# Router tiles transposed two chunks behind each product, their evacuation on ScalarE alone from tile 1 on, and SyncE's third weight load held until the first gather has landed

## What is computed

```python
def reference(x, mem, ...):
    mem_k, mem_v = project(_rms_norm(mem, norm_mem), xa_wkv)
    h = x
    for i in range(DEPTH):                                   # DEPTH = 2
        h = h + token_mixer(_rms_norm(h, norm_mix[i]))
        h = h + _memory_cross_attention(_rms_norm(h, norm_cross[i]), mem_k, mem_v, xa_wq[i], xa_wo[i])
        h = h + _hierarchical_moe(_rms_norm(h, norm_ffn[i]), moe_wg[i], moe_bg[i], moe_we[i], moe_be[i],
                                  moe_w1[i], moe_w3[i], moe_w2[i])
    return _rms_norm(h, norm_final)

def _hierarchical_moe(h, wg, bg, we, be, w1, w3, w2):        # 4 groups of 8 experts, D_EXPERT = 256
    g_logits = t @ wg + bg;  e_logits = t @ we + be
    # top-1 group, top-2 experts inside it, gate = softmax of the two times the group's probability
    for gi in range(G):
        hid = silu(t @ w1[gi]) * (t @ w3[gi]) * gate[gi]
        y = y + hid @ w2[gi]
```

## Time and profile before

| | us |
|---|---|
| median of 3 runs | 1807.48 (1802.3 to 1815.66) |
| the profiled execution | 1805.5 |
| its span, first to last instruction | 1803.6 |
| TensorE busy in the span | 1614.6 (90%) |
| VectorE, ScalarE, GpSimd busy | 708.1 (39%), 416.9 (23%), 164.5 (9%) |
| mean granted TensorE clock | 0.954 |

### The profile page before, as it was taken

The page is one execution under the profiler, slowest core; times in us unless marked ns, Lnnn a source line. Parts: engine busy times, 40 slices in busy tenths (PEclk is TensorE's granted clock), DMA queues, the critical chain, the costliest instruction groups (busy, mean ns, idle before and its releaser), DMA issues.

```text
span 1803.6 us, 26870 instructions
## 1 busy us (share of the span) xinstructions
PE 1614.6 (90%) x11581; PEld 845.2 (47%) x11581; DVE 708.1 (39%) x1308; ACT 416.9 (23%) x825; POOL 164.5 (9%) x185
## 2 busy tenths in 40 slices
PE   4999989998799999869887899999999996997876
PEld 2444458887464445434333344445544544333332
DVE  5310676664375215444221331205640454441215
ACT  2102335554300212211000120006511313010002
POOL 2000213330000000011111200000000000110101
PEclk8999999999799999879998999999999997998998
DMA  7119000000541611259999932211015025799994
GB/s 234 37 57 318 3 2 4 4 5 4 210 138 48 233 47 51 90 226 417 424 425 424 364 135 93 73 67 48 1 59 221 0 71 224 302 423 424 425 422 183
DMA packets 81496, 312.80 MB, mean 173 GB/s; under 512 B 17776, under 2 KB 18856, under 8 KB 56608
## 3 DMA queue, kind: packets, MB, share of 16 engines
q1 hardware_dynamic: 69280, 282.76, 40.0%
q0 software_dynamic: 10944, 24.10, 3.6%
q10 hardware_dynamic: 1152, 4.19, 0.6%
HBM read 305.81 MB, written 33.29 MB: 188 GB/s over the span
## 4 chain that ended last, share of the span: by engine, by line
PE 72%; issue 7%; DVE 4%; ACT 4%; DMA 1%; POOL 0%; another core or an unknown queue 0%; PEld 0%; DVEq 0%; ACTq 0%; POOLq 0%
PE PS L565 14%; PE PS L2269 14%; PE PS L605 10%; PE PS L1113 7%; PE PS L2294 6%; PE PS L579 5%; PE PS L1447 2%; PE PS L2254 2%; PE PS L2218 2%; PE PS L1423 1%; PE PS L1647 1%; PE PS L1668 1%; PE PS L504 1%; PE PS L1658 1%; PE PS L1814 1%
## 5 line engine op out<-in xcount | busy, mean ns | idle before, releaser
L565 PE MATMUL PS<-arena,ring 128*128 128x512 f32 (+1 forms) x1024 | 415.2, 567 | 0.0
L565 PEld LDWEIGHTS PS<-arena,ring 128*128 128x128 f32 x1024 | 195.4, 191 | 216.3 <-issue 210.7
L2269 PE MATMUL PS<-ring,arena 128*64 128x512 f32 x512 | 131.7, 673 | 50.8 <-issue 47.8
L605 PE MATMUL PS<-ring,arena 128*128 128x512 f32 x320 | 144.5, 602 | 0.7 <-ACT arena L1613 0.7
L2269 PE MATMUL PS<-arena 128*64 128x512 f32 x512 | 118.0, 614 | 15.0 <-issue 12.3
L2277 DVE TENSOR_TENSOR arena<-PS,arena 128x256 f32<-128x256 f32 x32 | 13.6, 424 | 249.6 <-PE PS L2284 231.0
L2269 PEld LDWEIGHTS PS<-ring,arena 128*64 128x64 f32 x512 | 43.6, 155 | 136.9 <-issue 133.2
L687 ACT ACTIVATE arena<-PS 128x512 f32<-128x512 f32 (+1 forms) x56 | 31.7, 566 | 307.7 <-PE PS L565 307.7
L2274 ACT ACTIVATE arena<-PS 128x256 f32<-128x256 f32 x32 | 12.3, 383 | 360.6 <-PE PS L2269 360.6
L605 PEld LDWEIGHTS PS<-ring,arena 128*128 128x128 f32 x320 | 60.9, 194 | 71.4 <-issue 70.5
L2269 PEld LDWEIGHTS PS<-arena 128*64 128x64 f32 x512 | 41.0, 142 | 90.4 <-issue 86.8
(11 more groups left out here) (317 smaller groups left out, 2124.3 us busy)
## 6 DMA issues: line engine op xcount, KB each, us to landing
arena<-in_moe_w SPq DMA_DIRECT2D x96, 1024.0 KB, 16.3
ring<-in_moe_w SPq DMA_DIRECT2D x96, 1024.0 KB
ring<-in_sb_wqkv SPq DMA_DIRECT2D x6, 2048.0 KB, 9.7
ring<-in_xa_wkv SPq DMA_DIRECT2D x4, 2048.0 KB, 16.0
ring<-in_xa_wq SPq DMA_DIRECT2D x4, 2048.0 KB, 8.5
ring<-in_xa_wo SPq DMA_DIRECT2D x4, 2048.0 KB, 13.6
h<-in_x SPq DMA_DIRECT2D x8, 512.0 KB, 5.2
ring<-in_rw_wr SPq DMA_DIRECT2D x2, 2048.0 KB, 14.7
```

Of the source, the lines that this page charges most:

```text
L565: ins = pe.matmul(PS[:, BANK_OF[g], 0:n], ring[:, u % RING, k, P * (j % 4):P * (j % 4) + P], xt[:, k, 0:n], start=(k == 0), stop=(k == KC ...
L605: ins = pe.matmul(PS[:, BANK_OF[g], :], rows(k), cols[:, k, :], start=(k == 0 and not grows), stop=(k == 3), skip_group_check=grows)
L2269: ins = pe.matmul(bank(2, 2, F)[r, :, :], xgT[p][:, k, r], w[a][:, :, k, :], start=(k == 0), stop=(k == KC - 1))
```

## The change

Three edits, the same in both layers. First, tiles 0, 1 and 2 are transposed two chunks after each of the four steps of groups 9, 11 and 12, in place of eight chunks after one step. Second, all chunks of tiles 1 and 2 are moved out by ScalarE, as those of tile 3 were, and for tiles 0, 1 and 2 ScalarE takes the sum of squares before it moves the chunks. Third, SyncE waits, ahead of the up weights of pair 2, until the first gather of the layer has landed.

```diff
--- before.py
+++ after.py
@@ -479,24 +479,19 @@
 
             return 5 + n % 3 if name[:3] == "ffn" else 4 + n % 4
 
+        def late_on_act(n):
+
+
+            return n % 2 == 0 or (LATE[n // (NT * KC)][:3] == "ffn" and n % (NT * KC) >= KC)
+
         def late_out(eng, n):
-
-            whole = [LATE0[m] + NT * KC - 1 for m in LATE if m[:3] == "ffn"]
-            if any(0 <= e - n < KC for e in whole):
-                eng.wait_ge(S("late_act"), late_counts(n)[0])
-            else:
-                eng.wait_ge(S("late_act" if n % 2 == 0 else "late_vec"), late_counts(n)[n % 2])
-
-        def late_counts(n):
-
-            act_too = [LATE0[m] + (NT - 1) * KC + k for m in LATE if m[:3] == "ffn" for k in range(1, KC, 2)]
-            moved = sum(m <= n for m in act_too)
-            return n // 2 + 1 + moved, (n + 1) // 2 - moved
-
-        def late_turn(pe, name, t, ready):
+            by_act = sum(late_on_act(m) for m in range(n + 1))
+            eng.wait_ge(S("late_act" if late_on_act(n) else "late_vec"), by_act if late_on_act(n) else n + 1 - by_act)
+
+        def late_turn(pe, name, t, ready, ks=range(KC)):
 
             ready(pe, t)
-            for k in range(KC):
+            for k in ks:
                 n = LATE0[name] + KC * t + k
                 depth = 3 if name[:3] == "ffn" else 4
                 if KC * t + k >= depth:
@@ -1449,10 +1444,18 @@
                         if m == 1:
                             ins.then_inc(S("proj_filled"), 1)
             ffn, ready = f"ffn{l}", h_tile_ready(xo)
+
+            def turns(n, t):
+
+                def quarter_turn(k):
+                    late_turn(pe, ffn, t, ready, (2 * k, 2 * k + 1))
+                    if (n, k) == (12, 1):
+                        route_logits(pe, l, 1)
+                    if (n, k) == (12, 3):
+                        route_ranks(pe, l, 0)
+                return {(n, k): lambda k=k: quarter_turn(k) for k in range(4)}
             seven_pe(pe, xo, oT, *XO_SUMS, lambda e, k: group_evacuated(e, FIRST[xv] + k),
-                     {(9, 1): lambda: late_turn(pe, ffn, 0, ready), (10, 1): lambda: route_logits(pe, l, 0),
-                      (11, 1): lambda: late_turn(pe, ffn, 1, ready), (12, 1): lambda: route_logits(pe, l, 1),
-                      (12, 2): lambda: late_turn(pe, ffn, 2, ready), (12, 3): lambda: route_ranks(pe, l, 0),
+                     {**turns(9, 0), **turns(11, 1), **turns(12, 2), (10, 1): lambda: route_logits(pe, l, 0),
                       (13, 1): lambda: route_logits(pe, l, 2), (13, 3): lambda: route_ranks(pe, l, 1)})
             late_turn(pe, ffn, NT - 1, ready)
             route_ranks(pe, l, NT - 2)
@@ -1867,9 +1870,12 @@
             for t in range(NT):
                 last = t == NT - 1
                 ready(act, t)
-                late_evac(act, name, t, xTE, 0, 1 if last else 2)
+                if last:
+                    late_evac(act, name, t, xTE, 0, 1)
                 end, total = 512 if last else C, sumsq[:, t:t + 1]
                 act.activation(tnE[:, t, 0:end], h[:, t, 0:end], ACT.Square, accum_out=total).then_inc(S("ffn_norm"), 1)
+                if not last:
+                    late_evac(act, name, t, xTE, 0, 1 if t else 2)
                 act.wait_ge(S("ffn_norm"), 9 * l + (1, 3, 5, 8)[t])
                 if last:
                     act.wait_ge(S("ffn_rstd"), 5 * l + 3)
@@ -1956,25 +1962,20 @@
                     vec.tensor_scalar(OS[:, t, k, :], iob, s8[:, m:m + 1], tokid[:, t:t + 1], ALU.is_equal, ALU.mult)\
                         .then_inc(S("onehots"), 1)
 
-            def evac(t):
-                late_evac(vec, f"ffn{l}", t, xTE, 1)
-
             vec.wait_ge(S("iota_ready"), 12)
             do(vec.tensor_copy(cum[:, 0, :], base))
             seven_sums(vec, xo, oT, *XO_SUMS, lambda e: group_evacuated(e, FIRST[xv] + KC - 1))
             add_group(vec, xo, 8, 0, 1)
-            evac(0)
+            late_evac(vec, f"ffn{l}", 0, xTE, 1)
             add_group(vec, xo, 9, 1, 1, 0, over=6)
             scale(0)
             group_and_first(0)
             add_group(vec, xo, 10, 1, 0, over=9)
             second(0)
-            evac(1)
             add_group(vec, xo, 11, 2, 1)
             scale(1)
             group_and_first(1)
             second(1)
-            evac(2)
             place(0)
             add_group(vec, xo, 12, 3, 1, 0, over=7)
             vec.wait_ge(S("ffn_norm"), 9 * l + 7)
@@ -2129,6 +2130,8 @@
 
             sp.wait_ge(S("rows_out"), 16 * NT * (l + 1))
             sp.wait_ge(S("logits"), NT * (l + 1))
+
+            sp.wait_ge(S("xg_in0"), 16 * (NPE // 2 * l + 1))
             for a in range(2):
                 load_up(sp, l, 4 + a, w13x[a], S("w13x_in"))
 
```

## The result

The changed kernel takes 1796.71 us (median of 9 runs, 1791.8 to 1798.71), the kernel before 1807.48 us (median of 9 runs by then, 1800.91 to 1815.66): a ratio of 0.994, with a 95% interval of 0.9919 to 0.9961. That is 10.8 us less, where 14 were forecast.

A forecast was written before the change was run, and what follows sets the result against it. Bound: the routing chain, VectorE and TensorE waiting in turn, then the first gather, ahead of a fixed-length weight stream. Gains of 8.4 and 5.9 us, rounded to 14, took the median from 1807.5 to 1793.5 us, range 1784 to 1803.

The forecast's parts named there:

- the sum: Gains over both layers: 8.4 us in layer 0 and 5.9 in layer 1, together 14.3, rounded to 14.
- Tile 0: Routing's tile 0, chunks between steps of group 9: 0.25 us gained per layer, between -0.5 and +0.7.
- The knot: Routing, add 10 to add 13, engines waiting in turn: shrinks to 20.95 us, gaining 6.1 (layer 0) and 3.6 (layer 1).
- the knot isn't VectorE's: Rival, routing: TensorE's written order keeps the chain long, only the gather's gain is left; 1803 us, chance 0.06.
- TensorE is late by its clock: Rival, groups 11 and 12: new waits bring half clock, gain falls by up to 7, 1800.5 us; 0.22 shared with gather rival.
- a sign of being wrong: Stated refutation sign: TensorE's clock reads 0.50 during groups 11 and 12 of the routing.
- The tail: Add 13 to the first gather: left unchanged at 14.74 and 16.01 us; either could move by up to 1.8 with the clock.
- the prediction's bound of 1.8 us: Limit on how far either layer's stretch from add 13 to the first gather could move with the clock.
- the clock stays up through the tail: Rival, logits 3 through up 0: denser TensorE work keeps full clock, giving back 1 to 3 us a layer; 1789, chance 0.20.
- The first gather: SyncE's wait shortens the gather by 2.1 us a layer (1.3 to 2.9), bringing up 0 and the stage's end forward equally.
- the gather gains little: Rival, first gather: gains 0 to 0.6 us a layer, not 2.1; 1797 us, chance 0.22 shared with late clock.
- The stream pushed back: Rival, expert stage: held pair 2 loads delay the weight stream; 1799 us partial, 1813 in full, chance 0.07.

The follow-up runs named there:

- e3: The changed kernel with tiles 0, 1 and 2 transposed in blocks of eight chunks again, ScalarE still moving tiles 1 and 2: 1793.82 us, ratio 0.9916.
- e6: The changed kernel with ScalarE moving each tile's chunks before it takes the squares, as before the change: 1800.96 us, ratio 0.9931.
- e4: The changed kernel with VectorE again moving the odd chunks of tiles 1 and 2, transposes still interleaved: 1802.43 us, ratio 0.9961.
- e5: The changed kernel with logits 1 one step earlier, ahead of chunk 3 of tile 2: 1794.92 us, ratio 0.9914.
- e2: The kernel before with only SyncE's wait for the first gather added: 1807.53 us, ratio 0.9991.
- e1: The changed kernel without SyncE's wait for the first gather: 1799.63 us, ratio 0.9943.
- e12: The kernel of e5 without SyncE's wait for the first gather: 1793.21 us, ratio 0.9907.
- e7: The changed kernel with SyncE's wait moved to the second gather, so the held loads start later: 1797.01 us, ratio 0.9936.
- e10: The changed kernel with three added unread products, one ahead of the last ranks and two in TensorE's wait for the first gather: 1798.09 us, ratio 0.9942.
- e11: The kernel of e5 with nine added unread products in TensorE's gaps from ranks 1 to the first gather: 1793.23 us, ratio 0.9899.

## Why the prediction was nearly right

It said 1793.5 us, 1784 to 1803, most likely within 1%; it is 1796.71, ratio 0.994. In the traces the edited part is 12.1 us shorter, where the sum had 14.3. The 2.2 us that are missing are made up of 0.8 more at tile 0, 0.4 less in the knot, 1.2 less in the tails, 0.3 in up 0, 2.1 in the stream, 1.3 in up 15, and 2.1 more ahead of the combination: the part up to add 13 is right, and what is missing lies behind it. The last 2.1 are luck, as said above; without them the traces would be 4.3 us short of the sum.

**Tile 0.** Booked 0.25 us a layer, came to 0.63 and 0.64 (12.01 to 11.38 and 11.37). It is the interleaving that gives it: with the chunks in blocks of eight (e3) the same stretch is 11.95. Squares first, which the prediction charges with a wait of 0.4 us, cost 0.25 there (e6 has 11.13).

**The knot.** Booked add 13 at 20.95 us behind add 10 in both layers, measured 21.23 and 21.11. Gains booked 6.1 and 3.6, measured 5.8 and 3.5. Its steps hold too: first 1 at 10.05 booked, 9.87 and 9.85 measured; TensorE's wait on ScalarE 1.7 booked, 1.60 and 1.58 measured; no wait of VectorE from first 1 to add 13 but the one for ScalarE's second half of the squares, which was in the sum. One term was added wrongly: first 2 is read as 2.77 us and stands in the sum as 2.6. With 2.77 the sum is 21.13. That the chunks on VectorE made it is shown by e4, that logits 1 were the next late thing by e5. What the prediction missed in it: it listed the wait, and the instruction queued behind it, and did not say that one of the three edits is a loss (e3: 1.8 us a layer in the knot, 1.2 net).

**The rival "the knot isn't VectorE's"** (1803) fell with e4. **"TensorE is late by its clock"** (1800.5): in layer 0 of after the clock is 1.00 in all of groups 11 and 12. In layer 1 it was at half for 3.4 us of group 12. The prediction called that a sign of being wrong, and yet add 13 came at 21.11 us, since the fall came behind logits 1 and the work under it was not what VectorE waited for. The rival is real where the fall comes earlier: e6 shows it in one layer, at 2.4 us.

**The tail.** Booked as unchanged. In layer 0 it grew from 14.74 to 16.12 us; in layer 1 it went from 16.01 to 15.87. Part of it is the clock after add 13, as the prediction's bound of 1.8 us allowed; logits 3 at half clock are one row of the chain:

```profile
771.91 3.63 PE PS L1817 x16
```

They took 2.76 us in the trace of before. The rival that the clock stays up through the tail, since TensorE's work is denser, did not come to pass: TensorE is through earlier and waits longer for VectorE's add 13, 2.68 us in after and 1.46 in before, and the clock is down behind that wait. That the longer wait makes the difference is argued, not shown.

**The first gather, the step that was mis-sized.** The prediction took 2.1 us a layer, and held that whatever brings the landing forward "brings up 0, the stream and the end of the stage forward by as much". The landing came forward by 2.53 and 1.72 us, 2.1 in the mean. The second half is the step that the runs do not bear out: e2, and the two pairs with and without the wait, put its worth for the whole kernel between nothing and 1.5 us a layer, so that 0 to 3 of the 4.2 us booked arrived. By what it is given back isn't shown. The rival "the gather gains little" gave the time nearly to the microsecond (1797), but for a wrong reason: the gather itself gained what was booked.

The Trainium skill, page "DMA: Bandwidth & Descriptors", section "Queues, rings and completion order", has the engines take turns between queues packet by packet; by that rule the weights would cost the gather about 1.2 us (an estimate from its half share). The traces show more: 1.2 to 2.6 us between the same layers with the wait and without (before and e2, e1 and after, e12 and e5), 1.8 in the mean. Only one of the six, layer 1 of e12 and e5, is as low as the estimate.

**The stream pushed back** (1799 to 1813). The loads fit with room to spare, as e7 shows. Yet in layer 1 of after the stream is 213.68 us and up 15 took 10.03 us in place of 8.78, together 2.9 more than before; it is one of the eight long streams above, and their cause is open.

## What to carry to other kernels

In a knot of engines that each keep a written order, write down for every wait what is queued behind it and who waits for that. Here eight chunks taken off VectorE were worth 3.9 us a layer (e4), and one small product put ahead of an instruction that waits was worth another 2.6. Look at each edit alone: spreading the chunks between the steps looked like a part of the gain and cost 1.2 us a layer, as long as logits 1 stood behind a chunk that waits (e5 moves them and has the shorter knot with the chunks spread). A landing that came 2 us sooner, ahead of a product at half clock and a stream of weights, was worth less than that here, for a reason not shown; a saving is safe only up to the next stage that has a length of its own.

## What the runs showed of the hardware

A gather of 0.5 MB takes 3.6 to 4.4 us from issue to its reader when it starts alone, with a second one 1.5 us behind, and 5.2 to 6.1 beside 4 MB of loads on another queue. After the clock's fall at the end of the product, three added products of 128x512 with pauses between them left it at 0.50 into up 0 in one layer of e10, and in the other it was back for 3.4 us, which ended as up 0 began. Nine of them, in a row of work with short pauses, brought it back (e11), and up 0 took 7.09 us in place of the 8.5 to 10.1 of all other layers. In after TensorE was busy for 4.00 of 4.00 us from 772 us on, at 0.50, and with the wait for the gather in between the clock stayed there until up 0 had run for 4.5 us. The same TensorE list has two lengths in the knot of the kernel before, 24.6 and about 26.3 to 27.0 us, with the layers' parts exchanged between two traces.
